# A hybrid decoder trunk on one core: one state for the linear attention, an opening in another order, three modulation steps moved

## The reference

```
c_act = silu(c)
mod = c_act @ ada_w[i] + ada_b[i]                  # 1024 x 6144 per layer
h = rms_norm(x, g) * (1 + sc) + sh
# GLA, 4 heads, DK = 128, DV = 256, four chunks of 64 tokens
q, k, v, r, glr = split(h @ w_in)
g = log_sigmoid(glr @ w_gate_up + b_gate) / 16;  G = cumsum of g inside a chunk
q_dec = q * exp(G);  k_inv = k * exp(-G);  k_tail = k * exp(G_last - G)
o_intra = (causal q_dec k_inv^T) v                 # inside a chunk
S_{n+1} = exp(G_last_n) * S_n + k_tail_n^T v_n     # state from chunk to chunk
o = o_intra + q_dec S
y = (rms_norm(o) * silu(r)) @ w_out;  x = x + gate * y
```

## Time and profile before

| | |
|---|---|
| median of 3 runs | 641.33 us |
| time of the profiled execution | 641.9 us |
| its span in the profile | 640.1 us |
| PE busy | 616.4 us (96%) |
| DVE busy | 474.3 us (74%) |
| ACT busy | 341.3 us (53%) |
| moved from DRAM | 156.40 MB, mean 244 GB/s |

### The profile page before, as it was taken

How to read it: one execution, slowest core, us unless ns; L and a number is a source line. 1 busy time by engine, 2 the same in 40 slices (tenths; PEclk the granted TensorE clock), 3 DMA queues, 4 the chain that set the end, 5 groups by cost and what they waited for, 6 DMA issues and landing times.

```text
span 640.1 us, 9098 instructions
## 1 busy us (share of the span) xinstructions
PE 616.4 (96%) x3393; PEld 515.5 (81%) x3393; DVE 474.3 (74%) x660; ACT 341.3 (53%) x581; POOL 39.3 (6%) x65
## 2 busy tenths in 40 slices
PE   3799999899999999999999999999999999999997
PEld 2477875677889988998977788888789899899985
DVE  3838998889768978979896898766786555455455
ACT  3446632668645345435558687666954443544440
POOL 3030020000000111101100000000000000000000
PEclk9699999999999999999999999999999999999999
DMA  9999499566588998999982655345376555556501
GB/s 333 387 356 392 150 357 380 215 247 248 193 278 319 373 364 315 388 337 333 355 295 108 226 197 194 132 133 171 128 260 227 179 177 181 192 192 197 197 0 66
DMA packets 59085, 156.40 MB, mean 244 GB/s; under 512 B 2835, under 2 KB 3329, under 8 KB 59057
## 3 DMA queue, kind: packets, MB, share of 16 engines
q1 hardware_dynamic: 47136, 112.34, 49.6%
q0 software_dynamic: 11760, 43.64, 19.1%
q10 hardware_dynamic: 160, 0.07, 0.0%
HBM read 154.98 MB, written 1.05 MB: 244 GB/s over the span
## 4 chain that ended last, share of the span: by engine, by line
PE 84%; DVE 10%; issue 2%; ACT 2%; DMA 1%; ACTq 0%; DVEq 0%
PE ps L501 14%; PE ps L503 14%; PE ps L502 14%; PE ps L700 7%; PE ps L699 7%; PE ps L698 7%; PE ps L508 4%; PE ps L510 3%; PE ps L509 3%; DVE w_lo L1435 1%; PE ps L629 1%; DVE spare L1435 1%; DVE ada_acc L1452 1%; PE ps L620 1%; PE ps L844 1%
## 5 line engine op out<-in xcount | busy, mean ns | idle before, releaser
L1051 ACT ACTIVATE w_hi<-w_raw 128x1024 fp32r<-128x1024 f32 x180 | 189.1, 1058 | 204.8 <-PE ps L503 106.9
L1435 DVE TENSOR_TENSOR w_lo<-w_raw,w_hi 128x1024 fp32r<-128x1024 f32 x180 | 218.0, 1222 | 96.5 <-ACT w_hi L1051 96.3
L700 PE MATMUL ps<-a_hi,w_lo 128*128 128x256 f32 x384 | 108.9, 284 | 0.0
L699 PE MATMUL ps<-a_lo,w_hi 128*128 128x256 f32 x384 | 108.9, 283 | 0.0
L698 PE MATMUL ps<-a_hi,w_hi 128*128 128x256 f32 x384 | 108.8, 283 | 0.0
L501 PE MATMUL ps<-w_hi,m_hi 128*128 128x512 f32 x256 | 100.4, 392 | 0.0
L502 PE MATMUL ps<-w_lo,m_hi 128*128 128x512 f32 x256 | 99.9, 390 | 0.0
L503 PE MATMUL ps<-w_hi,m_lo 128*128 128x512 f32 x256 | 99.8, 390 | 0.0
L501 PE MATMUL ps<-w_hi,a_hi 128*128 128x512 f32 x224 | 92.8, 414 | 4.6 <-DVE a_lo L1590 4.6
L503 PE MATMUL ps<-w_hi,a_lo 128*128 128x512 f32 x224 | 88.7, 396 | 0.0
L502 PE MATMUL ps<-w_lo,a_hi 128*128 128x512 f32 x224 | 88.5, 395 | 0.0
(11 more groups left out here) (204 smaller groups left out, 708.2 us busy)
## 6 DMA issues: line engine op xcount, KB each, us to landing
w_raw<-in_mlp_w_dram SPq DMA_DIRECT2D x64, 1024.0 KB, 5.5
ada_raw<-in_ada_w_dram POOLq DMA_DIRECT2D x40, 1024.0 KB, 6.7
w_raw<-in_gla_w_in_dram SPq DMA_DIRECT2D x12, 1024.0 KB, 13.2
w_raw<-in_moba_w_in_dram SPq DMA_DIRECT2D x12, 1024.0 KB, 7.4
ada_raw<-in_ada_w_dram SPq DMA_DIRECT2D x4, 1024.0 KB, 11.9
arena<-in_ada_w_dram SPq DMA_DIRECT2D x4, 1024.0 KB, 14.3
w_raw<-in_gla_w_out_dram SPq DMA_DIRECT2D x4, 1024.0 KB, 8.9
w_raw<-in_moba_w_out_dram SPq DMA_DIRECT2D x4, 1024.0 KB, 4.8
```

The source lines that it names most:

```text
L699: mm(o, w_hi[:, u, w], a_lo[:, a, :], start=False, stop=False)
L700: z = mm(o, w_lo[:, u, w], a_hi[:, a, :], start=False, stop=u == 3 and k == 1)
L1051: A(dst, w_raw[:, c // 2, c % 2], ACT.Copy).then_inc(hi_made, 1)
L1435: V.tensor_tensor(out, w_raw[:, c // 2, c % 2], w.bitcast(F32), ALU.subtract).then_inc(lo_made, 1)
```

## The change

**One state.** Instead of three states per head there is one, that after the first 128 tokens. `k_sum` is `k_tail` of chunk 1 beside `k_tail` of chunk 0 times the decay of chunk 1; one transpose per head turns it and one product of 128 rows per head gives the state, which ACT copies out of PSUM (`state_in`). The second half of a 128-token tile reads the first half by way of the scores: eight more products of 64x64 with `k_end`, and the mask `keep` is opened there. Queries of the last chunk are scaled by the decay of chunk 2.

**The opening.** ACT squares x first and does exp(-c) behind it with the table that is already there; DVE finishes silu(c) in three small operations. `angles` is cut in two: `pos_angles` (three operations) stays where it was, the rest stands behind the lo of the first four units. Memsets of `restart` and of `att` go from DVE to POOL.

**Places.** `masked` goes from (3, 3) to (4, 0), the updates and `turn_tail` to later places, `gated(1)` and `o_low` of the first two blocks ahead of unit (6, 3); ACT evicts `o_hi(0, 0)` and `o_hi(0, 1)` ahead of the last `read_in`. The modulation step of (3, 1) goes to (3, 0), one goes into (2, 1); three steps go from (5, 3), (6, 1) and the end of the GLA stage into the output projection, one ahead of each of its first three `lo`; `sum_mods` goes to (0, 2) and `turn_mods` to (1, 0).

```diff
-                            z = tr(ps[:, 2 + tb, h * DK:(h + 1) * DK], k_tailT[:, h, tile(tb)], eye[:, :])
+                    for h in range(GH):
+                        z = tr(ps[:, 2, h * DK:(h + 1) * DK], k_sumT[:, h, :], eye[:, :])
...
+                    for tb in range(TB):
+                        for h in range(GH):
+                            z = mm(ps[0:L, tb, h * P + L:(h + 1) * P], k_end[:, h, tb, :],
+                                   q_dec[:, h, tb * P + L:(tb + 1) * P], start=True, stop=True)
...
+                    for h in (2 * pair, 2 * pair + 1):
+                        z = mm(ps[:, 2 + pair, (h % 2) * DV:(h % 2 + 1) * DV], k_sum[:, h, :],
+                               g_v[:, 0, h * DV:(h + 1) * DV], start=True, stop=True)
...
+                            z = mm(o, att[:, tb, h, :], g_v[:, tb, h * DV:(h + 1) * DV], start=True, stop=tb == 0)
+                            if tb == 1:
+                                z = mm(o, q_dec[:, h, tile(1)], state[:, h, :], start=False, stop=True)
...
-                         {0: turn_k, 1: turn_q, 3: turn_tail},
-                         {0: scores, 2: lambda: update(0), 3: lambda: update(1)},
-                         {0: lambda: update(2), 1: lambda: update(3), 2: lambda: output(0), 3: lambda: output(1)},
+                         {0: turn_k, 1: turn_q},
+                         {0: turn_tail, 1: scores, 3: lambda: update(0)},
+                         {0: lambda: update(1), 2: lambda: output(0), 3: lambda: output(1)},
...
-                    out_project({0: lambda: turn_o(1), 3: lambda: sum_mods(1, 4)},
-                                {(0, 1): lambda: turn_mods(1, 5)})
+                    out_project({0: lambda: turn_o(1)},
+                                {(0, 2): lambda: sum_mods(1, 4), (1, 0): lambda: turn_mods(1, 5)})
...
-            nc.scalar.preload_act_table_set(SETS_SILU_SIN)
-            act.wait_ge(c_T, 1)
-            A(c_act[:, :], ps[:, 4, 0:KC], ACT.Silu).then_inc(c_ok, 1)
...
-                angles()
+                dve.wait_ge(c_e, 1)
+                link(V.tensor_scalar(c_act[:, :], c_act[:, :], 1.0, None, ALU.add))
+                link(V.reciprocal(c_act[:, :], c_act[:, :]))
+                V.tensor_tensor(c_act[:, :], c_act[:, :], ps[:, 4, 0:KC], ALU.mult).then_inc(c_ok, 1)
+                pos_angles()
...
                 for u in range(4):
+                    if u < 3:
+                        ada()
                     lo_at(mix_base[0] + 28 + u)
...
+                    V.tensor_tensor(k_sumT[:, :, 0:L], k_end[:, :, 0], dec[:, :, 1:2].to_broadcast([P, GH, L]),
+                                    ALU.mult).then_inc(kd_ok, 1)
...
-                    (2, 1): [logits], (2, 2): [cumulate], (2, 3): [keys], (3, 1): [queries, zero],
-                    (3, 3): [masked], (4, 1): [lambda: states(0)], (4, 2): [lambda: states(1)],
-                    (5, 0): [lambda: states(2)], (5, 1): [lambda: states(3)],
-                    (5, 3): [ada, o_scales, lambda: normed(0)],
+                    (2, 1): [logits, ada], (2, 2): [cumulate], (2, 3): [keys], (3, 1): [queries],
+                    (4, 0): [masked],
+                    (5, 3): [o_scales, lambda: normed(0)],
...
-                adas = [(2, 0), (3, 1), (3, 2), (4, 0), (4, 2), (5, 0), (5, 2), (6, 1)]
+                adas = [(2, 0), (3, 0), (3, 2), (4, 0), (4, 2), (5, 0), (5, 2)]
...
-                for _ in range(2):
-                    ada()
```

More of the change, by code:

```diff
@@ L368, in _ @@
             pool.wait_ge(pool_set, 2)
+            pool.wait_ge(pos_T, 1)
+            nc.gpsimd.memset(restart[:, :, :], 1.0).then_inc(restart_ok, 1)
+            pool.wait_ge(restart_ok, 1)
+            nc.gpsimd.memset(restart[:, :, 0:1], 0.0).then_inc(restart_ok, 1)
             pool.wait_ge(ada_pe, 6)
@@ L389, in _ @@
             for s in range(2, 4 * N_PAIRS_ADA):
+                if s == 5:
+                    pool.wait_ge(qd_ok, 1)
+                    nc.gpsimd.memset(att[:, :, :, :], 0.0).then_inc(zero_ok, 1)
                 pool.wait_ge(ada_mac, 2 * (s - 1))
@@ L1122, in first_norm @@
                     squares(0, tb)
+                act.wait_ge(c_T, 1)
+                A(c_act[:, :], ps[:, 4, 0:KC], ACT.Exp, scale=-1.0).then_inc(c_e, 1)
                 for i in range(2):
@@ L1189, in tail, with state_in @@
                     act.wait_ge(kt_p, 1)
-                    for tb in range(TB):
-                        z = A(k_tail[:, tb], ps[:, 2 + tb, :].rearrange("p (h d) -> p h d", h=GH), ACT.Copy)
-                    z.then_inc(kt_ok, 1)
+                    A(k_sum, ps[:, 2, :].rearrange("p (h d) -> p h d", h=GH), ACT.Copy).then_inc(kt_ok, 1)
+                def state_in(pair):
+                    act.wait_ge(u_p, pair + 1)
+                    A(state[:, 2 * pair:2 * pair + 2], ps[:, 2 + pair, :].rearrange("p (h d) -> p h d", h=2), ACT.Copy
+                      ).then_inc(st_ok, 1)
                 def o_squares(pair):
@@ L1226, in gla @@
                     (2, 3): [lambda: read_in(0, 1, [g_tok[:, 1, tb] for tb in range(TB)]), decays],
-                    (3, 2): [tail],
-                    (3, 3): [lambda: read_in(0, 2, [g_v[:, tb, 0:COLS] for tb in range(TB)])],
+                    (3, 3): [tail, lambda: read_in(0, 2, [g_v[:, tb, 0:COLS] for tb in range(TB)])],
+                    (4, 2): [lambda: state_in(0)],
                     (4, 3): [lambda: read_in(0, 3, [g_v[:, tb, COLS:D] for tb in range(TB)])],
+                    (5, 0): [lambda: state_in(1)],
                     (5, 2): [lambda: o_squares(0)],
@@ L1233, in gla @@
                              lambda: read_in(0, 4, [silu_r[:, tb, 0:COLS] for tb in range(TB)], ACT.Silu)],
-                    (6, 2): [lambda: read_in(0, 5, [silu_r[:, tb, COLS:D] for tb in range(TB)], ACT.Silu)],
+                    (6, 2): [lambda: o_hi(0, 0), lambda: o_hi(0, 1), lambda: read_in(0, 5, [silu_r[:, tb, COLS:D] for tb in range(TB)], ACT.Silu)],
                 }
@@ L1240, in gla @@
                             t()
-                for q in range(4):
+                for q in range(2, 4):
                     o_hi(0, q)
@@ L1546, in first_norm @@
                     modulate(0, slice(0, SEQ), 0, 0, (q,), lo_at)
-                V.memset(restart[:, :, :], 1.0).then_inc(restart_ok, 1)
-                dve.wait_ge(restart_ok, 1)
-                V.memset(restart[:, :, 0:1], 0.0).then_inc(restart_ok, 1)
                 for u in range(2, 4):
                     lo_at(u)
+                angles()
                 for i in range(2, 4):
@@ L1657, in queries @@
                     z.then_inc(qd_ok, 1)
-                def zero():
-                    dve.wait_ge(qd_ok, 1)
-                    V.memset(att[:, :, :, :], 0.0).then_inc(zero_ok, 1)
                 def masked():
                     dve.wait_ge(zero_ok, 1)
+                    dve.wait_ge(con_in, 32)
+                    V.memset(keep[0:L, L:P], 1).then_inc(keep_ok, 1)
+                    dve.wait_ge(keep_ok, 1)
                     dve.wait_ge(att_p, 1)
-                    dve.wait_ge(con_in, 32)
                     for tb in range(TB):
@@ L1724, in gla @@
                             ada()
-                o_low(0, range(2))
-                gated(1)
                 for i in range(2):
@@ L1918, in mlp, with pos_angles @@
                     residual(1, 1, 1, 1)
-            def angles():
+            def pos_angles():
                 H2 = HD // 2
@@ L1929, in angles @@
                 z.then_inc(pos_cp, 1)
+            def angles():
+                H2 = HD // 2
                 dve.wait_ge(pos_cp, 2)
```

70 lines of the change are left out of this document (32 added, 38 removed).

## The result

| | before | after |
|---|---|---|
| median of the runs, us | 641.71 (8 runs, 640.72 to 643.97) | 645.88 (8 runs, 643.72 to 647.50) |
| the profiled execution, us | 641.9 | 643.7 |
| its span, us | 640.1 | 641.9 |
| mean granted clock of PE in it | 0.991 | 0.989 |

The changed kernel is slower: ratio 1.0066, 95% interval 1.0050 to 1.0082, so 4.2 us. The forecast was 641.7, and its range ended at 644.9. The profiled execution is the fastest of the eight; the others are up to 3.8 longer, and their mean granted clock is lower (0.980 to 0.987). So there are two things to explain: why the profiled pair differs by +1.8 and not by the forecast's +0.4, and why the median lies 2.2 above the profiled execution.

The account below looks back on a forecast made before the run. PE, busy 616.4 of 640.1 us, bounds the kernel, so shifts of the first MLP's start reach the end. Terms -2.5 - 5.6 - 0.4 + 4.2 - 1.8 + 4.1 + 2.4 = +0.4 gave 641.7 us, range 638.4 to 644.9.

Parts of the forecast that it names:

- Parts 1 to 5: Terms from opening to output projection: -2.5, -5.6, +4.2, -1.8 ahead of the output projection, then +4.1 and +2.4 us.
- Opening: Before PE's first projection: x squared earlier and columns freed from the angles, so PE starts earlier; -2.5 us, at most 3.0.
- Idle time in the GLA stage: PE's waits there: 4.2 us more from the moved modulation step, while the existing hole of 0.39 goes.
- Idle time in the output projection: PE's waits: -1.8 for the earlier `a_lo`, +4.1 for later `turn_mods`, +2.4 us for the twelfth step.
- part 2: PE's own work in the GLA stage: fewer transposes, cheaper updates and outputs, more score products; -5.6 us, between -3.5 and -5.8.
- part 3: Modulation step ahead of the cumulative sum: its load lands 9.3 late, PE waits 4.2 us, or 1.8 with the load in time.
- the sum: All terms up to the first MLP added to +0.4 us, giving 642.3 for the profiled execution and a median of 641.7.
- Rival B: Output projection: waits of 2.4 and 4.4 bring down TensorE's clock, costing 2.7 more, 644.4 us; chance 0.16.
- estimate of 8.2 by even turns: Third modulation load at half of 388 GB/s while sharing with SP's queue: 8.2 us instead of 9.3; not adopted.
- Part 5: Output projection: later `turn_mods` delays residuals and norm by DVE's order, +4.1; lo behind the twelfth step, +2.4 us.
- A: Faster, GLA stage: third load is there when DVE comes to it, PE waits 1.8 instead of 4.2; 639.3 us, chance 0.30.
- C: Slower: opening gains only 0.5 instead of 2.5, as single-column products or modulation weights bind; 643.7 us, chance 0.12.

Follow-up runs that it names:

- fill_holes: Changed kernel plus unread products on PE, 9 and 15, in its two waits of the output projection; 641.98 us, ratio 1.0001 to the kernel before.
- after_again: The changed kernel measured once more with no edit; 646.78 us, ratio 1.0073 to the kernel before.
- sum_step_back: Changed kernel with the third modulation step back behind the queries, the three steps in the output projection kept; 643.78 us, ratio 1.0040 to the kernel before.
- small_loads: Changed kernel with POOL's first four modulation loads cut to an eighth of their columns, output not the reference's; 641.96 us, ratio 1.0006 to the kernel before.
- steps_back: Changed kernel with the last three modulation steps, `sum_mods` and `turn_mods` where the kernel before has them; 635.39 us, ratio 0.9906 to the kernel before.
- steps_back_old_open: steps_back with the opening of the kernel before; 638.28 us, ratio 0.9950 to the kernel before.
- gla_out_back: Changed kernel with every modulation step, `sum_mods` and `turn_mods` where the kernel before has them; 636.79 us, ratio 0.9933 to the kernel before.
- all_back_mods_behind: gla_out_back with the two residuals also ahead of `mods`; 636.51 us, ratio 0.9925 to the kernel before.

## Why the prediction was wrong

**Parts 1 to 5 held in size, term by term.** Opening -3.3 (forecast -2.5, at most -3.0; the first weights landed some 0.4 earlier than in the kernel before). PE's own work -5.9 (-5.6); of it `output` runs from 97.82 to 100.57, 2.75 in place of 4.63, and the second update pair takes 1.13 where 1.0 was forecast. Idle time in the GLA stage +3.1 (+3.8). Idle time in the output projection +4.8 (-1.8 + 4.1 + 2.4 = +4.7). They add to -1.3 in the profiled pair, where the forecast had +0.4. Two small slips in the forecast's own figures change nothing: the bounds of part 2 add up to -3.3 and -5.7, not -3.5 and -5.8, and part 3 with the load there in time gives a wait of 1.6, not 1.8.

**The step that failed is the sum: its term for the clock was nothing.** It took every product behind the new waits at the full clock, on the strength of one row: a hole of 1.77 that left the clock at 1.00. In the profiled execution the clock cost +2.9 of busy time in the output projection, and that turns -1.3 into +1.6; the first MLP starts at 155.11, where the forecast had 153.8. In the median it cost more. The sum took the median 0.6 below the profiled execution, as before, and it lies 2.2 above. Three places can bring the clock down behind the opening, in changing combinations and for 3.5 or 7 us: fill_holes, which removes it in the output projection alone, gives 4 to 5 us back.

Rival B had the mechanism and its place, at 0.16. It priced one fall at 2.7, which is what the long fall of after_again cost; that the two short falls of the first execution cost 2.9 together is a coincidence. And that fill_holes lands on the forecast is in part luck: the other terms came out 1.7 lower than forecast, and in its profiled execution a fall of the clock in the GLA stage and a first projection that starts 0.8 later (23.44) make up for it. A row with a hole of 1.77 says little on holes of 2.7 and 4.4, and the opening had shown that the clock can fall.

The Trainium skill, "TensorE: Matmul & The Clock Gate", "HAM oscillation", says that holes between matmuls throttle the clock again. These runs agree in direction, 0.50 at the holes of 2.70 and 4.34; but the hole of 2.63 in after_again left the clock at 1.00.

**Right in size, half wrong in cause: part 3.** The third load landed 9.6 after it was asked for (9.3 forecast). The estimate of 8.2 by even turns among the queues, worked out in the prediction from the Trainium skill, "DMA: Bandwidth & Descriptors", "Queues, rings and completion order", is shorter than that, and the trace stays with the longer figure. But in the kernel after DVE waits only 0.23 for that load; before, it has waited for the weights of block 2. The opening starts PE earlier and asks for the modulation loads earlier, and the same full DMA engines make the weights late. sum_step_back and small_loads show that both count: without the step a wait of 2.10 stays of the 3.4, without most of the early loads 1.04. So the size came out partly by luck.

**Part 5** was right, and incomplete: besides DVE's order the lo between the residuals waits for ACT, which stands behind `mod_rows`.

**Rivals.** A's condition nearly came, its consequence did not: the third load is there within 0.23, but DVE is late for another reason and PE has its holes in blocks 2 and 3. C did not come in this kernel, and did with the opening alone.

## What to carry to other kernels

A new wait in front of dense products (here 2.0 to 4.3 us) costs its own length and, in many executions, 1.4 to 2.7 us more for the products behind it, since the clock comes down; price both, for each such wait, before moving work towards the moments at which PE needs its result. When a trace shows one hole that the clock outlived, ask how long the new ones are. And where the DMA engines are full, an earlier start of one transfer is a later end of another: look for who stands first in the chain that the delayed one feeds (here the weights' landing went from 14.3 to 17.3).

## What had not been expected of the hardware

The same instruction stream, with waits equal within 0.1 us in the output projection (2.70 and 2.63, 4.34 and 4.35), had its clock brought down at both in one execution and at the second alone in another. Waits of 2.07 to 2.11 in the GLA stage left the clock at 1.00 in four profiles (the kernel after, steps_back, sum_step_back, steps_back_old_open), and one of 2.10 brought it to 0.50 in a fifth (fill_holes). A wait of 2.60 for `a_lo` left it at 1.00 in gla_out_back and brought it down in all_back_mods_behind. So the length of the hole alone does not decide; what does is open.
